# Seven block products in place of eight for queries and keys, with the weight sums on GpSimd and VectorE and part of the modulation moved behind the heads

## The reference, cut to what matters

```python
m = silu(cond) @ w_ada + b_ada                 # six rows of 2048 for each of the two conditions
h = rmsnorm(x) * (1 + scale1) + shift1
z = h @ w_in                                   # 12 heads of q, k, v (128 columns each) and 512 columns u
q, k = rmsnorm(q) * q_gain, rmsnorm(k) * k_gain
attn = softmax(q k' / sqrt(128) + bias) v      # windows for latent tokens, all keys for context tokens
ssm  = gated state space model of u
x1 = x + gate1 * (concat(attn, ssm) @ w_out)
y  = x1 + gate2 * experts(rmsnorm(x1) * (1 + scale2) + shift2)   # 16 experts, each takes its tokens
```

## Time and profile before

| | |
|---|---|
| median of three runs | 2381.94 us (2380.86 to 2382.67) |
| profiled execution, first to last instruction | 2381.9 us |
| outside the span, against the median | none that shows |
| the 12 head steps | 448.7 to 991.2 us |
| output projection and routing | 991.2 to 1325.6 us |
| experts | from 1325.6 us |
| busy: PE, DVE, ACT, POOL | 94%, 28%, 26%, 24% |

### The profile page before, as it was taken

One profiled execution on the slowest core, in us unless ns is written; L12 is line 12 of the kernel. 1 busy time (PEld: TensorE's weight loads), 2 busy tenths in 40 slices (PEclk: granted clock), 3 DMA queues, 4 the chain that ended last, 5 costly groups with the idle time before them and its releaser, 6 DMA issues.

```text
span 2381.9 us, 57827 instructions
## 1 busy us (share of the span) xinstructions
PE 2249.8 (94%) x25901; PEld 1478.5 (62%) x25901; DVE 673.6 (28%) x1172; ACT 611.4 (26%) x1400; POOL 573.4 (24%) x638
## 2 busy tenths in 40 slices
PE   5999999999999999999997689999999999999997
PEld 3468888666665656544443666666776666666663
DVE  4124442367776775320114100000000000000001
ACT  3011111365655664210035121111111111111100
POOL 0246771476676675000000100000000000000000
PEclk9999999999999999999999799999999999999998
DMA  9922322865656464321433989999999999999995
GB/s 370 371 86 58 89 55 65 203 208 178 197 190 205 159 198 139 149 87 73 154 124 158 341 336 401 409 410 409 409 408 413 410 422 410 392 409 406 408 407 193
DMA packets 184087, 625.67 MB, mean 263 GB/s; under 512 B 14574, under 2 KB 91160, under 8 KB 154156
## 3 DMA queue, kind: packets, MB, share of 16 engines
q1 hardware_dynamic: 165240, 581.91, 63.7%
q0 software_dynamic: 3424, 20.97, 3.4%
q10 hardware_dynamic: 15188, 19.19, 2.4%
HBM read 597.59 MB, written 24.44 MB: 261 GB/s over the span
## 4 chain that ended last, share of the span: by engine, by line
PE 72%; DMA 12%; DVE 5%; issue 4%; ACT 2%; POOL 1%; SPq 1%; ACTq 1%; DVEq 0%; POOLq 0%
PE PS L1776 20%; PE PS L1603 11%; PE PS L1512 11%; PE PS L1790 10%; PE PS L1326 8%; DMA work<-in_w_gate 8%; DMA hT_<-in_w_gate 3%; PE PS L1268 3%; PE PS L1203 3%; POOL work L2448 1%; DVE PS L2132 1%; PE PS L1498 1%; PE PS L1230 1%; DMA work<-in_w_ada 1%; PE PS L1833 1%
## 5 line engine op out<-in xcount | busy, mean ns | idle before, releaser
L1776 PEld LDWEIGHTS PS<-hT_,work 128*64 128x64 f32 x14336 | 512.3, 140 | 101.8 <-issue 91.9
L1776 PE MATMUL PS<-hT_,work 128*64 128x80 f32 x14336 | 531.5, 235 | 43.4 <-issue 28.6
L1512 PE MATMUL PS<-hT_,work 128*128 128x512 f32 (+1 forms) x1536 | 433.2, 434 | 0.0
L2448 POOL TENSOR_TENSOR work<-work 128x512 f32<-128x512 f32 x240 | 305.1, 1271 | 162.5 <-ACT work L1004 146.9
L1512 PEld LDWEIGHTS PS<-hT_,work 128*128 128x128 f32 x1536 | 226.3, 192 | 146.9 <-issue 146.8
L1790 PE MATMUL PS<-work,hT_ 128*32 128x512 f32 (+1 forms) x2544 | 302.1, 599 | 2.5 <-DMA work<-in_w_down 1.8
L1603 PE MATMUL PS<-work,mixT_ 128*128 128x512 f32 x640 | 281.8, 595 | 0.0
L1173 ACT ACTIVATE hT_<-PS,small 128x64 f32<-128x64 f32 x248 | 102.6, 414 | 676.7 <-PE PS L1203 676.7
L2303 DVE TENSOR_TENSOR hT_<-PS,hT_ 128x480 f32<-128x480 f32 x16 | 10.5, 658 | 856.5 <-ACT hT_ L1182 856.5
L1326 PE MATMUL PS<-work,hT_ 128*128 128x256 f32 x960 | 213.0, 380 | 1.8 <-DMA work<-in_w_in 1.8
L2498 POOL DMA_INDIRECT out_y<-mixT_,work x15 | 22.0, 1466 | 793.4 <-DVE mixT_ L2330 793.4
(11 more groups left out here) (306 smaller groups left out, 1890.1 us busy)
## 6 DMA issues: line engine op xcount, KB each, us to landing
work<-in_w_up SPq DMA_DIRECT2D x57, 2048.0 KB, 26.6
work<-in_w_down SPq DMA_DIRECT2D x56, 2048.0 KB, 32.4
work<-in_w_gate SPq DMA_DIRECT2D x55, 2048.0 KB, 31.1
work<-in_w_ada SPq DMA_DIRECT2D x48, 2048.0 KB, 10.1
work<-in_w_in SPq DMA_DIRECT2D x80, 512.0 KB, 6.2
hT_<-in_w_gate SPq DMA_DIRECT2D x9, 2048.0 KB, 33.6
work<-in_w_out SPq DMA_DIRECT2D x4, 4096.0 KB, 13.4
hT_<-in_w_down SPq DMA_DIRECT2D x8, 2048.0 KB, 29.7
```

The costliest lines, as they stand in the source:

```text
L1512: last = pe.matmul(qk_bank(which)[:, (ctx_at if ctx_ else lat_at)[which]], w_chunk[chunk % NW][:, HD * (k % 8):HD * (k % 8) + HD], hT[:, k ...
L1776: last = pe.matmul(hidden_at(u, f)[64 * h:64 * h + 64, :], w[:, k % 4, f // 2, f % 2, 64 * h:64 * h + 64], xsT[s][:, k, :], start=opens, s ...
L2448: TT_(acc_ctx[p % 3], acc_ctx[p % 3], prod[i % 3], ALU.add).then_inc(s_padd, 1)
```

## The change

Per head, eight block products become seven, of eight matmuls each, all on 320 tokens. Sums of token blocks (`S1` to `S4`) are made once by DVE. Sums of weight blocks are made for each head: POOL makes `T1` and then overwrites one raw block (`near_weights`), DVE makes `T2` and `T4`. The products add up in three PSUM banks, and between two products in one bank DVE takes out what stands there (`combine`, five times a head). Late modulation is cut to 12 blocks a step (144 in all), loaded one by one through three buffers instead of eight at a time, and the 112 others go behind the heads, between the tiles of the output projection, where ACT issues their loads. `w_out` comes in halves of eight row tiles. The bias rows `spans`, once loaded for all heads, are loaded for two heads at a time, by 16 DMAs. The norm chain, slots and experts stay.

```diff
-LATE_STEP = 24
+LATE_STEP = 12
+LATE_HEADS = LATE_STEP * HEADS
+LATE_SUMS = {3: 0, 6: 1, 8: 2, 11: 3}
...
+            def product(h, b, weights, tokens, ks, starts, done):
                 for k in ks:
+                    last = pe.matmul(product_bank(b), weights[:, HD * k:HD * k + HD], tokens[:, k, :],
+                                     start=(starts and k == 0), stop=(k == 7), skip_group_check=True)
+                if done:
+                    last.then_inc(s_part, 1)
...
             def step(h):
                 g = h - 1
+                p1(h, range(0, 5))
                 if g >= 0:
                     key_sums(g)
+                p1(h, range(5, 8))
+                p6(h)
+                p2(h, range(0, 4))
                 slot(g, 0)
                 if g >= 0:
                     key_rows(g)
+                p2(h, range(4, 8))
+                p7(h, range(0, 2))
                 slot(g, 1)
+                if h in LATE_SUMS:
+                    pe.wait_ge(s_root, h)
+                    late_sums(LATE_SUMS[h], 4)
+                p7(h, range(2, 8))
                 slot(g, 2)
+                context_key(h)
+                p4(h, range(0, 6))
+                slot(g, 3)
+                p4(h, range(6, 8))
+                p5(h, range(0, 4))
+                slot(g, 4)
+                p5(h, range(4, 8))
+                p3(h, range(0, 2))
+                slot(g, 5)
+                p3(h, range(2, 8))
+                slot(g, 6)
+                query_sums(h)
```

`p1` and `p2` go to bank 0, `p6`, `p7` and `p4` to bank 1, `p5` and `p3` to bank 2. `p7` waits for `combine(h, 1)`, `p4` for `combine(h, 2)`, `p3` for `combine(h, 4)`, and `combine(h, 3)` finishes the second half of the queries behind `p4`. DVE's step, SP's loop over the heads, and what DVE and ACT do between the output tiles:

```diff
             def step(h):
+                g, more = h - 1, h < HEADS
+                if g >= 0:
+                    combine(g, 5)
+                late(h, 0, 2)
...
                 if g >= 0:
                     normed(g)
+                if more:
+                    combine(h, 1)
+                slot(g, 0, 2)
+                late(h, 3, 1)
+                slot(g, 1, 4)
...
+                    fourth_weights(h)
+                    combine(h, 2)
+                slot(g, 2, 5)
+                late(h, 6, 1)
+                slot(g, 3, 7)
+                if more:
+                    combine(h, 3)
+                slot(g, 4, 8)
+                late(h, 9, 1)
+                if more:
+                    combine(h, 4)
                 slot(g, 5)
+                if h + 1 < HEADS:
+                    second_weights(h + 1)
                 slot(g, 6)
+                if more:
+                    query_sums_turned(h)
+                late(h, 10, 2)
...
             for h in range(HEADS):
+                first = LATE_STEP * h + 3
+                if h:
+                    for n in (4 * h + 3, 4 * h + 4):
+                        if RAW <= n < 4 * HEADS:
+                            head_block(n)
...
+                for m in range(first + 8, first + 12):
+                    if m < LATE_HEADS:
+                        late(m)
+                if h % 2 and h + 1 < HEADS:
+                    head_spans((h + 1) // 2)
                 if 1 <= h < HEADS - 1:
                     head_cache(h + 1)
...
+            def late_steps(m, n):
+
+                for m in range(m, m + n):
+                    late_step(m)
+                    if m + 3 >= LATE_HEADS + 4 and m + 3 < LATE_ALL:
+                        act.wait_ge(s_prod, m)
+                        act.wait_ge(s_lated, m)
+                        act.dma_start(late_ring[late_slot(m + 3)], late_source(m + 3)).then_inc(s_late[late_slot(m + 3)], 16)
```

More of the change, by code:

```diff
@@ L180, in trunk_step @@
         at(sources_end)
-        A1, A2 = [take(2560) for _ in range(2)]
+        A2, A1 = [take(2560) for _ in range(2)]
         BT = take(2048).rearrange("p (e n) -> p e n", e=16)
@@ L556, in ring @@
                     src, k = w_in_v[:, 2 * n:2 * n + 2, 3 * D_ATTN:3 * D_ATTN + D_SSM], 2
[L557 removed]
+                else:
                     job, part = n // 4 - 2, n % 4
@@ L982, in key_rows, with roots @@
+            def roots(g):
+                act.wait_ge(s_kss, g + 1)
+                act.activation(rstd[:, 0:N_LAT], bank(4), ACT.Sqrt, bias=eps[:, :], scale=1 / HD)
+                act.activation(rstd[:, N_LAT:TOK], ctx_sums, ACT.Sqrt, bias=eps[:, :], scale=1 / HD)
+                act.wait_ge(s_qst, QST + g + 1)
+                act.activation(query_rms, turned_sums, ACT.Sqrt, bias=eps[:, :], scale=1 / HD).then_inc(s_root, 1)
             def key_rows(g):
@@ L1524, in sums_free, with p3, query_sums @@
+            def p3(h, ks):
+                if 0 in ks:
+                    block_landed(4 * h + 2)
+                    pe.wait_ge(s_sums, SUMS + 3)
+                    pe.wait_ge(s_comb, combined(h, 4))
+                product(h, 2, raw[(4 * h + 2) % RAW], S4, ks, False, 7 in ks)
+            def query_sums(h):
+                pe.wait_ge(s_qhalf, 2 * h + 2)
+                if h:
+                    pe.wait_ge(s_root, h)
+                rows = sum(at_ <= h for at_ in LATE_SUMS)
                 if rows:
@@ new lines, in _ @@
+            out_tile(0, 2, range(4, 8))
+            slot(last_head, 3)
+            pe.wait_ge(s_lated, LATE_HEADS)
+            out_tile(0, 3, range(0, 4))
+            slot(last_head, 4)
+            out_tile(0, 3, range(4, 8))
+            slot(last_head, 5)
+            pe.wait_ge(s_late_row, len(LATE_SUMS))
+            out_tile(0, 4, range(0, 4))
+            slot(last_head, 6)
+            out_tile(0, 4, range(4, 8)).then_inc(s_wdone, 1)
+            w_out_landed(1)
+            for tt in range(TT):
+                out_tile(0, tt, [k for k in range(8, MIX_T) if k != last_head])
@@ L1638, in shifts_summed @@
                 pe.wait_ge(s_router, ROUTER + 1)
-                pe.matmul(bank(6, 32), ones, shift1[:, :], start=True, stop=True).then_inc(s_columns, 1)
+                pe.matmul(bank(7, 32), ones, shift1[:, :], start=True, stop=True).then_inc(s_columns, 1)
             def turned_block(i):
@@ L2439, in _, with late @@
                     phases(m + 1)
-            def late(h):
-                for m in range(LATE_STEP * h, min(LATE_STEP * h + LATE_STEP, 16 * 16)):
+            def late(first, n):
+                for m in range(first, first + n):
                     p, k = m // 16, m % 16
```

792 lines of the change are left out of this document (476 added, 316 removed).

## The result

The changed kernel takes 2388.72 us (median of 20 runs, 2383.53 to 2396.35) against 2381.88 us (20 runs) of the kernel before on the same chip: a ratio of 1.0025, 95% interval 1.0016 to 1.0033. That is slower, and by a little more than the 0.2% that can be told from no change (the interval reaches down to 0.16%), on the side to which the prediction gave 0.17, and outside its range. The profiled execution is 2391.0 us long.

The account below looks back on a forecast made before the run. PE was taken to bound heads and output projection, the weight stream the experts. 53.0 + 7.2 - 8.3 - 1.4 - 8.0 - 23.5 - 1 - 3 = 15.0 us saved from 2381.9 gave 2367 us, range 2341 to 2387.

Parts of the forecast that it names:

- the side to which the prediction gave 0.17: Whole kernel: the outcome slower than the kernel before, chance 0.17, against 0.66 for faster and 0.17 for same.
- Products, +53.0: Heads: seven products of 320-column matmuls at 0.269 us each save 4.42 us a head, 53.0 us over 12 heads.
- Waits recovered, +7.2: Heads: PE's 12 waits on scaled probabilities, 7.2 us in all, go because fewer late blocks stand between slots.
- Additions behind `p5`, -9.7: Between `p5` and `p3`, PE waits for DVE's addition: 8.3 us over 11 steps, plus 1.4 in step 0.
- Key sums, -8.0: End of a head: PE's key sums wait 0.73 us for ACT's squares in 11 steps, costing 8.0 us.
- the rival of a late POOL: Heads: POOL's two weight sums take 3.3 us each, not 2.7; 16 us lost, 2383 us, no change; chance 0.15.
- Blocks behind the bias rows, -23.5: `p2` in steps 2, 4, 6, 8, 10 waits 4.7 us for a block issued behind 16 bias loads: 23.5 us.
- The rival in which the blocks are in time: Heads: short issues cost little and blocks land in some 3 us, so the five waits vanish: 2343 us; chance 0.20.
- waits at the end of a head: Heads: the step pricing PE's waits for DVE's additions (-8.3, -1.4) and for ACT's squares at the key sums (-8.0).
- First half of `w_out`, -1: Start of the output projection: 2 MB asked for 6.7 us ahead lands in 7.7, costing 1 us.
- Late blocks behind the heads, -3: Output projection: 112 late blocks at 1.26 us fit, chain at 163 against PE's 182; 3 us taken for shared engines.
- third rival: Output projection: late blocks hold PE because loads share DMA engines; above 1.43 us a block; 27 us, 2394; chance 0.15.

Follow-up runs that it names:

- experiment 4: Changed kernel with slot 5 put between `p5` and `p3` instead of two matmuls into `p3`: 2391.27 us, 1.0034 to the kernel before.
- experiment 1: Changed kernel with the 16 bias-row loads issued mid-step, no longer ahead of the block that `p2` needs: 2363.64 us, 0.9922 to the kernel before.
- experiment 2: Changed kernel with the context key put three matmuls into `p4`, no longer directly behind slot 2: 2381.27 us, 0.9994 to the kernel before.
- Experiment 6: Changed kernel with the late sums of pair 5 made two tile halves later: 2391.56 us, 1.0036 to the kernel before.
- experiment 5: Changed kernel with the 108 late loads on ACT cut to 64 of 512 columns (results partly wrong): 2379.32 us, 0.9987 to the kernel before.
- the fastest kernel: Kernel of experiment 8, with SP asking for one expert piece only when late block 254 is done: 2336.03 us, 0.9815 to the kernel before.
- experiment 8: Changed kernel, bias rows and context key moved, gate-row wait and pair 5 sums later, slot 5 before `p3`, key sums behind all `p1`: 2341.37 us, 0.9824.

## Why the prediction was wrong, step by step

- **Products, +53.0.** The price is right, 0.269 us each; the saving itself is checked by the balance below.
- **Waits recovered, +7.2.** Right, none of them is left; from start to start they were 9.2 (at 748.00 before, a stop of 0.81 us has 0.64 in its row).
- **Additions behind `p5`, -9.7.** Nearly right: 13 waits, 8.7 us by their rows and 11.0 from start to start. It is the only price of the product that stands directly behind the one in whose bank it adds. It is also a price that can't be had back alone (experiment 4).
- **Key sums, -8.0.** Size nearly right (6.9 in 11 by the rows, 9.9 from start to start), cause incomplete. The text ends the chain at DVE's addition and gives POOL's sums 0.5 us of cover. ACT's squares stand behind POOL, 0.4 us later than DVE's addition would let them start, and experiment 4 shows that POOL keeps them there. POOL's sums themselves are shorter than assumed (2.35 and 2.45 us against at most 2.7), so the rival of a late POOL did not come as told.
- **Blocks behind the bias rows, -23.5.** Right in size: 24.5 by experiment 1, 22.2 by the steps. But that is in part luck, two errors that cancel: the block of step 4 lands in 4.4 us, not 6.2, so the five waits are 2.9 to 3.4 us and not 4.7, and three of them are followed by 1.8 us of slower matmuls, which the sum had not. The rival in which the blocks are in time is out.
- **A wait that the prediction doesn't have, 8.9.** Under "waits at the end of a head" only the product banks were gone through. The bank that slot 2 shares with the context key was not: before, other matmuls stood behind that product. This step failed too, as a term left at nothing. It costs 0.8 us a step by its rows, 10.8 us in all from start to start; 7.4 by experiment 2.
- **First half of `w_out`, -1.** Measured 2.2, with slower matmuls behind it: 5.32 us for eight, which take 3.60 elsewhere.
- **Late blocks behind the heads, -3.** This step failed most: the overlap of the late chain with PE. "It fits" rested on a mean pace: 1.26 us a block, a load of 2.9 us, and a chain ready 19 us early. The median load is indeed 3.1 us. The forecast of PE's side was also short: its 75.5 us to the sum that needs block 191 are those of 88 matmuls at 0.86 (though the text says 40 + 80 and 8), and there are 92 and the sum of pair 4, 80.3 us. The chain was there after 90.4 us, not 69.5. For the loads that meet 2 MB of SP's take 7 or 8, and ACT, which multiplies and issues in order, stands for each: 6.0 us at 1039.90, 4.6 at 1107.17. Experiment 6 shows when the chain ends: 202 us after the last slot, where PE without waits is at 190 (experiment 5), not 182; the chain was forecast for 163. By the prediction's own formula p = (202 - 22) / 112 = 1.61, above the 1.43 at which its third rival decides. That rival, with 0.15, is what came, at about 12 us and not 27. (Its 2394 counts the 3 us of the sum and its own 27 together; with the 27 in place of the 3 it is 2391.)

ACT in order of time, the second of these waits in the changed kernel, and SP's load ahead of it:

```profile
1098.05 0.38 SPq L720 DMA_DIRECT2D work<-in_w_out  x1
...
1101.89 0.72 ACT L1094 ACTIVATE work<-work,cT 128x512 f32<-128x512 f32 x1 [0.62 <-POOL work L2740]
1107.17 0.72 ACT L1094 ACTIVATE work<-work,cT 128x512 f32<-128x512 f32 x1 [4.56 <-DMA work<-in_w_ada]
```

What stands between heads and experts adds up so: late sums of four pairs moved out of the heads 4.0, `w_out` 2.2 and 1.7 of slower matmuls, pair 5 10.0 and 2.1 behind it (sums of 1.86 us that take 1.00 elsewhere, and 70.11 us for 160 matmul instructions that take 68.87 in experiment 5): 20.0 of 21.0 us.

The heads add up too, from start to start: 53.0 for the products, 9.2 recovered, 4.0 for the late sums that moved out, less 11.0, 9.9, 22.2 and 10.8, is 12.3 us, and 12.7 were measured. So nothing larger than 0.4 us is missing, and the products gave what was forecast.

Against the sum of 15.0: 10.8 for the slot's bank, 1.2 + 1.7 for `w_out`, 9.1 more than the 3 for the late blocks; the other four terms together are off by 0.1. That leaves -7.7, with the measured medians at -6.8.

The direction turned on the slot's bank and the late blocks, together 20 us. What stays open: when a wait is followed by a slow stretch and when not, the last 4 us of wait at pair 7 in the fastest kernel, and what it would cost to keep all late blocks in the heads, which no run tried.

## What to carry to other kernels

Where many small loads feed a chain that another engine will wait for, go through the large loads that another queue asks for in that time, one by one; here a single one held the chain up by 4.6 to 6.0 us, and a median landing time doesn't show that. When a product moves, go through every PSUM bank next to its new place, not only the bank it writes. Give a wait of PE of some 3 us a second, higher price (half as much again in three of five cases here, nothing in two), and try an edit that removes a wait together with cover for the wait that follows it: slot 5 alone brought nothing, with later key sums the two brought 15 us.

## What the runs showed of the hardware

- PE after a wait of 3.32 us: eight 320-column instructions in 3.95 us, not 2.16; after one of 3.35 us, two steps later, in 2.26. Ahead of `w_out`'s first half a wait of 2.11 us (experiment 1) was followed by 5.40 us for eight instructions of 512 columns, and one of 2.48 us (experiment 8) by 3.70. So the length of the wait alone doesn't tell. After 10.0 us: late sums of 1.06 us each, not 0.62, at a granted clock of 0.53 over ten microseconds, nearer to the lower of its two levels (1.2 and 2.4 GHz) than to the upper.

```profile
1110.00:1120.00 10.00, 5.07 (x13) 1.74 (x14) 6.05 (x9) 5.59 (x9) 9.05 (x8) 0.53 0.80 247
```

- Two additions of 128x1024 from SBUF, on DVE and POOL at once: the one that starts second ends about its own length behind the first (DVE 3.17 us against a mean of 1.23 for the same line in experiment 4, where it starts first; POOL 3.38 against 2.35). By the Trainium skill ("SBUF — State Buffer", Who interferes with whom) a DVE `tensor_tensor` with both inputs in SBUF and GpSimd's reads shut each other out; both rows agree.
- 256 KB on ACT's queue land in 3.1 us (median of 108); two that met 2 MB on SP's took 7 to 8 us. The Trainium skill ("DMA: Bandwidth & Descriptors", Issuing engines are not separate DMA queues) says that both run on the same 16 DMA engines; these rows agree.
